# Seven quarter-size products for seven more projection tiles of a two-layer decoder trunk

## What is computed

```
layer 0:  x += silu(layernorm(depthwise_conv(glu(rms(x) @ w_in)))) @ w_out + b_out
layer 1:  x += (gated linear attention over q, k, v, r = rms(x) @ gla_w_in) @ gla_w_o
both:     x += cross_attention(rms(x) @ w_q, keys and values of 256 memory tokens) @ w_o
          x += mixture of 32 experts, two per token, of rms(x)
end:      rms(x)
```

## Time and profile before

| | |
|---|---|
| median of 3 runs | 1863.63 us (1862.57 to 1864.18) |
| profiled execution | 1863.45 us, span of its trace 1861.6 us |
| granted TensorE clock, mean | 0.989 of full |
| busy | TensorE 98%, VectorE 35%, ScalarE 20%, GpSimd 12% |
| conv output, two tiles | TensorE from 244.58 to 299.5 us |
| layer 0 queries to attention output | 299.51 to 451 us |
| expert stages | 459.7 to 942.8 and 1360.9 to 1844 us |
| linear attention | 942.8 to 1200.75 us |
| layer 1 queries to attention output | 1200.75 to 1352.6 us |

### The profile page before, as it was taken

One profiled execution on the slowest core, in us unless ns is written; L12 is line 12 of the kernel. 1 busy time (PEld: TensorE's weight loads), 2 busy tenths in 40 slices (PEclk: granted clock), 3 DMA queues, 4 the chain that ended last, 5 costly groups with the idle time before them and its releaser, 6 DMA issues.

```text
span 1861.6 us, 19144 instructions
## 1 busy us (share of the span) xinstructions
PE 1821.4 (98%) x7748; PEld 963.8 (52%) x7748; DVE 647.3 (35%) x1264; ACT 378.6 (20%) x670; POOL 219.7 (12%) x176
## 2 busy tenths in 40 slices
PE   7999999998999999999998999999989999999997
PEld 6445744545454444444476875455454544444443
DVE  3899121234132222222337423213232322322224
ACT  2334221221111111111135123122121111111112
POOL 0566201011000000000063210200100000000001
PEclk9999999998999999999999999999989999999998
DMA  9215432022899999999951204202069999999993
GB/s 363 74 42 181 142 130 91 2 92 91 337 419 418 420 421 419 419 419 420 416 186 46 91 0 181 114 22 94 6 281 417 419 420 420 420 419 420 417 421 153
DMA packets 90603, 477.58 MB, mean 257 GB/s; under 512 B 7758, under 2 KB 8188, under 8 KB 40972
## 3 DMA queue, kind: packets, MB, share of 16 engines
q1 hardware_dynamic: 89164, 470.88, 62.6%
q0 software_dynamic: 736, 3.15, 0.6%
q10 hardware_dynamic: 608, 2.24, 0.3%
HBM read 472.05 MB, written 4.19 MB: 256 GB/s over the span
## 4 chain that ended last, share of the span: by engine, by line
PE 89%; DVE 8%; issue 1%; ACT 1%; DMA 1%; POOL 0%; SPq 0%; POOLq 0%; DVEq 0%; ACTq 0%
PE PS L726 24%; PE PS L505 14%; PE PS L754 11%; PE PS L534 7%; PE PS L785 7%; PE PS L768 7%; PE PS L461 5%; DVE PS L2020 5%; PE PS L1048 3%; PE PS L555 2%; PE PS L635 1%; PE PS L544 1%; PE PS L775 1%; PE PS L740 1%; PE PS L797 1%
## 5 line engine op out<-in xcount | busy, mean ns | idle before, releaser
L1894 DVE TENSOR_TENSOR xT<-PS,xT 128x512 f32<-128x512 f32 x256 | 161.2, 684 | 239.9 <-PE PS L768 239.9
L726 PE MATMUL PS<-ring,xg 128*64 128x512 f32 x1024 | 226.8, 595 | 0.0
L726 PE MATMUL PS<-ring,hT 128*64 128x512 f32 x1024 | 226.3, 595 | 0.0
L505 PE MATMUL PS<-hT,ring 128*128 128x512 f32 x512 | 222.1, 593 | 0.7 <-DVE hT L1986 0.7
L754 PE MATMUL PS<-ring,hT 128*64 128x512 f32 x960 | 212.6, 595 | 0.0
L505 PEld LDWEIGHTS PS<-hT,ring 128*128 128x128 f32 x512 | 96.7, 190 | 119.2 <-issue 118.3
L726 PEld LDWEIGHTS PS<-ring,hT 128*64 128x64 f32 x1024 | 70.9, 137 | 135.4 <-issue 134.2
L726 PEld LDWEIGHTS PS<-ring,xg 128*64 128x64 f32 x1024 | 70.7, 137 | 135.0 <-issue 133.8
L754 PEld LDWEIGHTS PS<-ring,hT 128*64 128x64 f32 x960 | 66.3, 137 | 130.4 <-issue 129.4
L1922 DVE TENSOR_TENSOR ylo<-PS,yhi 128x1024 fp32r<-128x1024 f32 (+1 forms) x32 | 38.1, 1191 | 229.9 <-ACT yhi L1458 223.1
L2020 DVE SCALAR_TENSOR_TENSOR PS<-RU,R,PS 128x512 f32<-128x512 f32 x168 | 111.3, 750 | 0.0
(11 more groups left out here) (302 smaller groups left out, 1959.3 us busy)
## 6 DMA issues: line engine op xcount, KB each, us to landing
ring<-in_moe_w_gate SPq DMA_DIRECT2D x128, 1024.0 KB, 12.1
ring<-in_moe_w_up SPq DMA_DIRECT2D x128, 1024.0 KB, 13.5
ring<-in_moe_w_down SPq DMA_DIRECT2D x128, 1024.0 KB, 9.8
ring<-in_xa_w_kv SPq DMA_DIRECT2D x16, 1024.0 KB, 7.3
ring<-in_gla_w_in SPq DMA_DIRECT2D x12, 1024.0 KB, 9.6
ring<-in_conv_w_in SPq DMA_DIRECT2D x8, 1024.0 KB, 14.7
ring<-in_xa_w_q SPq DMA_DIRECT2D x8, 1024.0 KB, 7.4
ring<-in_xa_w_o SPq DMA_DIRECT2D x8, 1024.0 KB, 14.1
```

The costliest lines, as they stand in the source:

```text
L505: mm = pe.matmul(bank(b), w[:, k * 512 + m * P:k * 512 + (m + 1) * P], src[:, k, :], start=(k == 0), stop=(k == C - 1))
L726: mm = pe.matmul(PS[e * SL:(e + 1) * SL, kind * BANK:(kind + 1) * BANK], x[:, k, (2 * (p % 2) + e) * SL:(2 * (p % 2) + e + 1) * SL], ring[ ...
L1894: dve.tensor_tensor(xT[:, c, :], bank(XBANK + b), xT[:, c, :], ALU.add).then_inc(g[f"x_read{b}"], 1)
```

## The change

All seven tiles `conv_out` 0 and 1, `xq` 0 and `xo` 1 of both layers, and `gla_o` 1 are computed by `product`. Their sums of weights and inputs are added to the queues of GpSimd and VectorE. Where the result is a residual, VectorE adds all seven products to `xT` (bank plus SBUF) and writes the gained chunks after (`gained`); the bias of the conv output is added to `xT` early by ScalarE. The chunk order of these norms becomes `ORDER`. The moves in linear attention: the copies of v tile 0's products 6 and 7 go ahead of `decays(0)`, the addition of its product 5 ahead of `staged(1)`, and product 1 of r tile 0 ahead of `scores(0)`. The ring gets the mixing slots twice in layer 0 and three times in layer 1. The core of the diff:

```
+        mixed_co = [Mixed(0, "conv_out", i, i, 0, (2 * i, 2 * i + 1), False) for i in range(2)]
+        mixed_o = Mixed(1, "gla_o", 1, 10, 4, (6, 7), False)
+        mixed_xq = [Mixed(l, "xq", 0, (2, 11)[l], (1, 5)[l], (4, 5), False) for l in range(DEPTH)]
+        mixed_xo = [Mixed(l, "xo", 1, (3, 12)[l], (2, 6)[l], (5, 6), False) for l in range(DEPTH)]
...
 TensorE, attention(l)
-                query(0)
-                norm_sums(ni)
-                query(1)
-                query(2)
+                product(u, 1, hT, lambda k: wait_h(pe, ni, k))
+                product(u, 2, hT, lambda k: wait_h(pe, ni, 4 + k))
+                product(u, 6, hT)
+                product(u, 7, hT)
+                pe.wait_ge(norm_sum, ni - 1)
+                token_sums(("rs", ni), [dg[:, :, :].rearrange("p t s -> p (t s)")], 0)
+                for j in (5, 4, 3):
+                    product(u, j, hT)
+                plan.next = 6
+                query(4)
...
 TensorE, xo(l, w)
+                product(u, 1, oT)
+                product(u, 2, oT)
+                turn_h(0)
+                product(u, 6, oT)
+                turn_h(1)
+                logits(0)
+                for j in (7, 5, 4, 3):
+                    product(u, j, oT)
+                project_chunk(w, 2, ("xo", l, 2), oT, b=0)
...
 TensorE, conv output and gla_o
+            product(mixed_co[0], 1, sT, lambda k: pe.wait_ge(silu_ready, k + 1))
+            product(mixed_co[0], 2, sT, lambda k: pe.wait_ge(silu_ready, 4 + k + 1))
+            for j in (6, 7, 5, 4, 3):
+                product(mixed_co[0], j, sT)
+            for j in (1, 2, 6, 7, 5, 4, 3):
+                product(mixed_co[1], j, sT)
...
-            w = tile(1, "gla_o", 1, ("go", 7))
-            for m in range(4):
-                go_part(4 + m, (6, 7, 2, 3)[m], range(0, 8))
+            for j in (1, 2, 6, 7, 5, 4, 3):
+                product(mixed_o, j, qT)
...
 GpSimd, layer 1, then layer 0
+                    mix_first(mixed_o)
                     pool.wait_ge(*full(("gt", C - 1)))
                     pool.dma_start(RK[:, 0:2 * C * NMEM], spill).then_inc(s_back, 16)
+                    mix_first(mixed_xq[1])
+                    mix_last(mixed_o)
...
+                    mix_first(mixed_co[0])
+                    mix_first(mixed_co[1])
+                    mix_last(mixed_co[0])
+                    mix_first(mixed_xq[0])
+                    mix_last(mixed_co[1])
+                norm_adds(2 + 3 * l)
+                mix_last(mixed_xq[l])
+                mix_first(mixed_xo[l])
...
 VectorE, end of linear attention
-            residual(("go",), 5)
+            for c in range(C):
+                dve.wait_ge(*read(("gt", c)))
+            mix_x_first(4, 1, qT)
+            mix_x_rest(4, 1, qT)
+            for c in range(4):
+                residual(("go",), 5, c)
+            for j in (1, 2, 6, 7, 5, 4):
+                added(mixed_o, j, xT)
...
 VectorE, xo(l), behind the copies of values(3) and four casts
+                mix_x_first(u.src, l, oT)
+                mix_x_rest(u.src, l, oT)
+                residual(("xo", l), ni, 0)
+                residual(("xo", l), ni, 1)
+                added(u, 1, xT)
...
 VectorE and ScalarE, v tile 0
             staged(0)
+            added(mixed_v[0], 5, vG)
             staged(1)
-            added(mixed_v[0], 5, vG)
...
+            copied(mixed_v[0], 6, vG)
+            copied(mixed_v[0], 7, vG)
             decays(0)
-            copied(mixed_v[0], 6, vG, 1, 0)
             decays(1)
-            copied(mixed_v[0], 7, vG, 1, 1)
```

More of the change, by code:

```diff
@@ L114, in weight_tiles, with four @@
     kv1 = [("kv1", i) for i in range(4)]
[L115 to L118, removed]
+    def four(first, second, n):
+        return [(first, 0), (first, 1), (second, 0), (second, 1), ("mix_x", n), ("mix_w", n)]
+    layer0 = kv0[:1] + conv + kv0[1:] + kv1 + [("conv_out", 0), ("conv_out", 1), ("mix_x", 0), ("mix_w", 0)]
+    layer0 += four("xq", "xo", 1)
+    layer1 = four("gla_in", "gla_v", 0) + four("gla_r", "gla_o", 1) + four("xq", "xo", 2)
     return [layer0, layer1]
@@ L539, in product, with transposes @@
                     release[n] = key
[L541 to L542 removed]
+            def transposes(key, pairs, b=None):
+                b = take(key, b)
                 for j, src in enumerate(pairs):
@@ L669, in turn_h @@
                     wait_h(pe, ni, c)
[L670 to L682, removed]
+                    transposes(("ht", l, c), [hT[:, c, t * P:(t + 1) * P] for t in range(TT)], HT_BANK[place(ni, c)])
+                u = mixed_xo[l]
+                product(u, 1, oT)
[7 more added lines that the diff above has]
+                project_chunk(w, 2, ("xo", l, 2), oT, b=0)
+                turn_h(6)
+                turn_h(7)
+                logits(6)
+                turn_h(4)
+                project_chunk(w, 3, ("xo", l, 3), oT, b=1)
+                turn_h(5)
+                logits(4)
+                logits(2)
+                turn_h(2)
+                plan.next = 4
                 norm_sums(ni)
@@ L1696, in norm_recip, with gained @@
                 link(dve.reciprocal(rrec, rstat))
[L1698 removed]
+            def gained(i, c):
+                wait_x(dve, i, c)
                 name, g0 = norm_gain[i]
[L1700 to L1712 removed]
@@ L1949, in xo @@
                     link(dve.tensor_copy(d, src[:, :]))
-                residual(("xo", l), 3 + 3 * l, after=lambda c: low(l, c))
+                u, ni = mixed_xo[l], 3 + 3 * l
+                for c in range(C):
+                    dve.wait_ge(*read(("o", l, c)))
+                mix_x_first(u.src, l, oT)
[3 more added lines that the diff above has]
+                added(u, 1, xT)
+                added(u, 2, xT)
+                low(l, 0)
+                added(u, 6, xT)
+                low(l, 1)
+                added(u, 7, xT)
+                added(u, 5, xT)
+                added(u, 4, xT)
+                gained(ni, 6)
+                gained(ni, 7)
+                added(u, 3, xT)
+                gained(ni, 4)
+                gained(ni, 5)
+                residual(("xo", l), ni, 2)
+                low(l, 6)
+                low(l, 7)
+                low(l, 4)
+                residual(("xo", l), ni, 3)
+                low(l, 5)
             dve.wait_ge(s_constp, NCONST)
```

316 lines of the change are left out of this document (187 added, 129 removed).

## The result

The changed kernel takes **1848.88 us** in the median of 4 runs (1848.27 to 1851.64), beside 1863.89 us (1862.57 to 1864.18, 4 runs) of the kernel before on the same chip: ratio 0.9927, 95% interval 0.9913 to 0.9940. The forecast was 1853 us, 1840 to 1862.

A forecast was written before the change was run, and what follows sets the result against it. TensorE, busy 98% of the span, was taken as the bound. Terms -23.2 - 8.7 + 4.0 + 4.0 + 4.7 + 9.1 gave -10.1 us, from 1863.45 to about 1853 us, range 1840 to 1862.

The forecast's parts named there:

- seven tiles: TensorE's work: each tile computed by seven products saves 3.32 us, seven tiles -23.2 us.
- v tiles: Linear attention's v tiles: 12.3 us of losses go, new waits of 2.8 and 0.75 us come, net -8.7 us.
- wait at conv output: Conv output: GpSimd's weight sums hold up VectorE's eight scalings, so product 1 starts late, +4.0 us.
- wait in the linear output: Linear output projection: input sums interleave with GpSimd's weight sums, so product 6 waits, +4.0 us (3.2, or 4.8 if copies suffer).
- waits at attention output: Attention output, both layers: product 1 waits for a residual behind the input sums, 2.3 and 2.4 us, +4.7 us.
- clock, conv and linear output: The two 4.0 us waits each make the clock fall, 9.1 us at half speed, 4.55 lost each, +9.1 us.
- router: Router stages: taken as not touched by the change, no term in the sum.
- Product 1 takes bank 5, which holds chunk 1: Attention output: the bank step behind the forecast waits of 2.3 and 2.4 us, +4.7 us together.
- chunk, transposes, logits, norm, keeps its shape: End of the attention output stage, ahead of the router: order unchanged, no cost forecast.
- A wait of 2.83 us at 10.9 to 13.7 left it at full: Clock evidence from the trace of before: waits of 2.3 to 2.8 us should not lose the full clock.
- rival that the clock survives a wait of 4 us: Waits come but the clock survives one or both: 1849 us with one fall, 1844 with none; chance 0.32 together.
- rival in which it falls in every new wait: Clock falls in all five new waits, 5 us lost each: 1868 us, slower than before; chance 0.08.

The follow-up runs named there:

- experiment 5: Changed kernel with GpSimd's three weight sums of the second conv output tile moved after the last sum of the first: 1846.70 us, ratio 0.9904.
- experiment 6: Changed kernel with GpSimd's weight sums of layer 1's query tile made right after those of the linear output tile: 1845.21 us, ratio 0.9904.
- experiment 3: Changed kernel with the attention output tile of each layer in matrix banks 1 and 6 in place of 5 and 6: 1858.10 us, ratio 0.9968.
- experiment 4: Changed kernel with the router's running count in matrix bank 0 in place of the next in turn, bank 6: 1847.59 us, ratio 0.9914.
- experiment 2: The kernel before, run again without an edit for its profile: 1863.38 us, ratio 0.9999.
- the changed kernel's repetition: The changed kernel run again without an edit, in another session: 1852.17 us, ratio 0.9940.

## Why the prediction came out

The sum of the forecast was -10.1 us, and the rest of the span measures -11.4 (first profiles) or -11.3 (means of two). It is no proof of its steps. Two were missed, with opposite signs, and two more were mis-sized, again with opposite signs; that the errors nearly cancel is luck.

| step | forecast | measured | from |
|---|---|---|---|
| seven tiles | -23.2 | -23.2 | queries -3.30, -3.29; attention output -3.34, -3.35; conv output -6.59 (experiment 5); linear -3.29 (experiment 6) |
| v tiles | -8.7 | -6.6 | 46.80 to 40.19 us |
| wait at conv output | +4.0 | +3.8 | waits |
| wait in the linear output | +4.0 (3.2 to 4.8) | +4.9 | waits |
| waits at attention output | +4.7 | 0 | experiment 3 |
| clock, conv and linear output | +9.1 | +5.2 | 6.54 - 3.77 and 7.32 - 4.86 |
| router | 0 | +4.5; +3.6 by two profiles of each kernel; +2.6 by experiment 4 | first profiles: 22.40 and 22.36 us in place of 20.14 and 20.10, from the norm's sums to the first product of the experts |
| sum | -10.1 | -11.4 | rest of the span, first profiles: -11.4 |

**Right.** A tile saves 3.3 us. GpSimd's sums and VectorE's instructions with two SBUF inputs take turns, so that the scalings take 10.9 us (the forecast had them start at 236.1 and end at 247.1), and the wait behind them has the forecast's place and releaser. In the v tiles the old wait goes and the order of VectorE puts one of 2.84 (2.8) and one of 0.64 (0.75) in its place.

**The failed step** is "Product 1 takes bank 5, which holds chunk 1". It rested on reading how banks are handed out, and not on a row; experiment 3 shows that the wait is there, 4.6 us, when the bank is the one that I thought it was. **The missed step** is of the same kind: the forecast says of the end of that stage that "chunk, transposes, logits, norm, keeps its shape", and it does, but the bank that comes next in turn behind it had become another one, held by a transpose whose reader stands behind the router's searches (experiment 4).

**Mis-sized** is the clock: 4.55 us for each fall, from one row with a low clock of 10.2 us. It was low for 6.8 us at both places, and those cost 2.8 and 2.5. By the forecast's own signs ("Half clock shows for 10 us after each 4 us wait", and wrong "if the clock reacts otherwise") this step did not come true.

**A misread row.** The forecast also took the 2.8 us wait in the v tiles as one that keeps the clock, because "A wait of 2.83 us at 10.9 to 13.7 left it at full". The row doesn't show that. Its 1.00 stands for a stretch without any record of the clock (experiment 2), and the products behind that wait ran at the rate of the lower level until 18.9 us; the row itself has six of them in 2.31 us, nearly 0.39 each, in place of 0.216. Whether the clock fell in that wait or had been low before it, that trace does not say; in six of the other profiles a fall is on record at this place, in the changed kernel's repetition at 14.51 us, 1.2 us behind a wait of 2.06. So nothing in the trace of before spoke against a fall behind 2.8 us, and it came: of the seven profiles that have this wait it kept it in two and lost it in five, for 3.4 us, 1.8 us of time each. Of the seven with the wait of 3.8 at the conv output six lost the clock; the two of 2.1 and 2.5 us (experiment 3) kept it. The rival that the clock survives a wait of 4 us (0.32) was thus no idle one: it came in one profile of seven. The rival in which it falls in every new wait came true in part, at a smaller price. The range of 1840 to 1862 us held with both sessions inside.

**The open bound.** For the linear output the trace of before left 3.2 to 4.8 us, by whether VectorE's gained copies, with one SBUF input, are held up too. They are: one took 2.14 us in place of 0.49 beside GpSimd's last sum, and the wait was 4.86. The Trainium skill (GPSIMD Engine Reference, Key points) names VectorE's two-port modes as contending with GpSimd; the forecast read the copies as such, and by that reading this term would have been 4.8, as measured, though the sum of all terms would have come out 0.8 us further off. An addition with one input in PSUM took 0.68 us beside GpSimd's last sum, as it does alone.

The Trainium skill (TensorE: Matmul & The Clock Gate, What's actually happening) says that the number of slow matmuls at the start of one and the same kernel differs from run to run, with the phase of the clock gate. The traces agree: the kernel before had twelve slow products in its first profile and none in its second, the changed kernel none and eight.

What stays open is what decides in one execution whether the clock falls behind a wait of 2.8 or 3.8 us, and how long it stays low.

## What to carry to other kernels

When work is taken from TensorE and put on VectorE and GpSimd, list for each of their large instructions what the other one does in that stretch, and move the ones that aren't due: here three moves of existing work (the two weight sums, and the addition in the v tiles) were worth more than the change's own net gain, and the last of them only when GpSimd was held back too, since an earlier product releases an earlier sum. Follow buffers that are handed out in turn through the whole program after an edit of the order, the untouched stages too, with their readers; print the assignment rather than derive it. Profile each version more than once before a few us are explained, since the start alone varied by 4 us in code that nobody had touched. And where a profile gives the clock as full, check it against the spacing of the products: a stretch without a record reads as full.

## What the hardware showed that I had not expected

- Both sides pay: beside VectorE's input sums GpSimd's own sums grew from 2.36 to 3.21 and 3.32 us, and VectorE's from 1.22 to 3.3. At the conv output the forecast had GpSimd keep its 2.36 us for each sum; the two beside the scalings took 2.68 and 2.79. The Trainium skill (SBUF — State Buffer, two separate sides) speaks of a lock that either engine holds for a whole instruction while the other stands, which agrees with these rows.
- After waits that were the same to 0.1 us the low clock lasted differently: 0 or 3.4 us behind 2.8, 0 or 6.8 behind 3.8, 3.4 or 6.8 behind 4.9, and 10.2 or 13.7 in a router with a wait of 6.9.
- The clock at the start of the program alone moves the whole time by up to 2.8 us: none to thirteen of the first 64 products ran at the rate of the lower level, and the 64 took 14.05 to 16.87 us.
